# Summing the second layer's modulation with GpSimd beside a dense feed-forward

## The reference, cut to what matters

```python
c_act = jax.nn.silu(c)
for layer in range(DEPTH):                                   # DEPTH = 2
    mod = c_act @ mod_w[layer] + mod_b[layer]                # 1024 x 6144
    sh_m, sc_m, gt_m, sh_f, sc_f, gt_f = jnp.split(mod[:, None, :], N_MOD, axis=-1)
    h = x * (1 + sc_m) + sh_m
    ...                                                      # mixers (S5, GLA), w_out
    x = _layer_norm(DN_ALPHA * x + (1 + gt_m) * y, ln_mix_g[layer], ln_mix_b[layer])
    h = x * (1 + sc_f) + sh_f
    ...                                                      # layer 0: dense feed-forward; layer 1: 8 experts
    x = _layer_norm(DN_ALPHA * x + (1 + gt_f) * f, ln_ffn_g[layer], ln_ffn_b[layer])
```

## Time and profile before

| what | value |
|---|---|
| runs, not profiled | 2794.58 us median of 3 (2790.40 to 2800.55) |
| the profiled execution, first to last instruction | 2788.6 us |
| PE busy in it | 2530.0 us (91%) |
| DVE busy | 2080.7 us (75%) |
| ACT busy | 1461.2 us (52%) |
| POOL busy | 18.0 us (1%), 24 of its 29 instructions in the mixers |
| mean granted TensorE clock | 0.948 |

### The profile page before, as it was taken

How to read it: one execution, slowest core, us unless ns; L and a number is a source line. 1 busy time by engine, 2 the same in 40 slices (tenths; PEclk the granted TensorE clock), 3 DMA queues, 4 the chain that set the end, 5 groups by cost and what they waited for, 6 DMA issues and landing times.

```text
span 2788.6 us, 32539 instructions
## 1 busy us (share of the span) xinstructions
PE 2530.0 (91%) x12413; PEld 2026.9 (73%) x12413; DVE 2080.7 (75%) x2254; ACT 1461.2 (52%) x1535; POOL 18.0 (1%) x29
## 2 busy tenths in 40 slices
PE   5989689998686999999999999998888999988998
PEld 2736567777455788888888888876777887767787
DVE  5588787665766899989898988997865554776554
ACT  1221433442233777777777787775544544454543
POOL 0001000000000000000000000000000000000000
PEclk9997899998697999999999999999989999999999
DMA  7451246654132899999999999995403553503452
GB/s 239 154 184 66 91 171 250 243 211 127 46 121 76 307 356 360 347 361 356 345 361 372 371 358 355 359 348 191 139 31 106 166 187 110 196 1 106 136 183 89
DMA packets 274343, 598.12 MB, mean 214 GB/s; under 512 B 28722, under 2 KB 37248, under 8 KB 273026
## 3 DMA queue, kind: packets, MB, share of 16 engines
q1 hardware_dynamic: 252144, 580.30, 58.7%
q10 hardware_dynamic: 22034, 15.67, 2.0%
HBM read 594.87 MB, written 1.06 MB: 214 GB/s over the span
## 4 chain that ended last, share of the span: by engine, by line
PE 64%; DVE 26%; ACT 4%; issue 2%; ACTq 2%; DMA 2%; DVEq 0%; POOLq 0%
PE PS L215 62%; DVE WL L171 6%; PE PS L237 2%; DVE MW L171 2%; DVE WF L171 2%; DVE AR L171 2%; ACTq L150 2%; ACT WH L207 2%; DVE MOD L171 1%; DVE HF L171 1%; DVE H L171 1%; DVE SMALL L182 1%; DVE AR L179 1%; DVE HTR L171 1%; ACT AR L207 1%
## 5 line engine op out<-in xcount | busy, mean ns | idle before, releaser
L171 DVE TENSOR_TENSOR WL<-RG,WH 128x1024 fp32r<-128x1024 f32 (+1 forms) x558 | 919.2, 1647 | 371.2 <-ACT WH L207 339.0
L207 ACT ACTIVATE WH<-RG 128x1024 fp32r<-128x1024 f32 (+1 forms) x558 | 781.7, 1401 | 615.4 <-PE PS L215 552.7
L215 PE MATMUL PS<-WH,HTR 128*128 128x512 f32 (+2 forms) x2920 | 847.6, 388 | 40.9 <-DVE HTR L171 13.7
L215 PEld LDWEIGHTS PS<-WH,HTR 128*128 128x128 f32 x2920 | 551.3, 191 | 154.5 <-DVE HTR L171 15.3
L215 PE MATMUL PS<-WL,HTR 128*128 128x512 f32 (+2 forms) x1460 | 506.8, 385 | 1.4 <-DVE WL L171 1.4
L215 PE MATMUL PS<-WH,ATR 128*128 128x512 f32 x1624 | 457.9, 394 | 17.5 <-DVE WL L171 9.4
L215 PEld LDWEIGHTS PS<-WH,ATR 128*128 128x128 f32 x1624 | 305.9, 189 | 82.6 <-DVE WL L171 16.0
L215 PE MATMUL PS<-MW,HTR 128*128 128x512 f32 x1332 | 330.0, 395 | 1.0 <-DVE MW L171 0.5
L215 PEld LDWEIGHTS PS<-WL,HTR 128*128 128x128 f32 x1460 | 279.0, 191 | 55.5 <-DVE WL L171 2.7
L215 PEld LDWEIGHTS PS<-MW,HTR 128*128 128x128 f32 x1332 | 244.5, 188 | 55.3 <-DVE MW L171 6.5
L171 DVE TENSOR_TENSOR MW<-RG,MW 128x2048 fp32r<-128x2048 f32 x112 | 256.8, 2292 | 12.5 <-ACT MW L207 0.6
(11 more groups left out here) (230 smaller groups left out, 1993.9 us busy)
## 6 DMA issues: line engine op xcount, KB each, us to landing
RG<-in_moe_w_gate SPq DMA_DIRECT2D x112, 1024.0 KB, 6.9
RG<-in_moe_w_up SPq DMA_DIRECT2D x112, 1024.0 KB, 6.7
RG<-in_moe_w_down SPq DMA_DIRECT2D x112, 1024.0 KB, 6.8
RG<-in_w_ff SPq DMA_DIRECT2D x64, 1024.0 KB, 5.0
RG<-in_mod_w SPq DMA_DIRECT2D x48, 1024.0 KB, 5.2
RG<-in_w_in SPq DMA_DIRECT2D x34, 1024.0 KB, 6.1
RG<-in_w_out SPq DMA_DIRECT2D x16, 1024.0 KB, 5.1
RG<-in_ffn_w_gate SPq DMA_DIRECT2D x14, 1024.0 KB, 5.2
```

Of the source, the lines that this page charges most:

```text
L171: return self.did(lambda: self.e.tensor_tensor(o, a, b, op))
L207: return self.did(lambda: self.e.activation(o, a, f, bias=bias, scale=scale))
L215: return self.did(lambda: self.e.matmul(o, l, r, start=start, stop=stop))
```

## The change

- `plan_sums` now plans 24 raw loads, i = 0..11 with two k each: i 0 to 3 are columns 0:2048, i 4 to 7 columns 3072:5120, i 8 to 11 the two gate rows. `SUMS_BY` puts one pair behind gate n and one pair behind up n in each of the blocks 1 to 6.
- The eight loads (`plan_mod(1, 6, 10)`), the 64 matmuls, the ACT copy, the transposes and DVE's finish of them leave the second mixers.
- `g_sums` runs on POOL beside the feed-forward. For each load it multiplies the ring slot in place by c_act[k] (tensor_scalar) and adds the slot to the sum (tensor_tensor). In the first load of columns one multiplication writes the sum itself. For the gate rows both steps are done twice, on 1024 columns each.
- DVE does no sums any more. PE's 16 matmuls of one column come twice, in blocks 3 and 6 (`COLUMNS_BY`), and DVE adds the bias (`v_sums`) before the low parts of down n-1; ACT's part (`a_sums`) is gone. POOL waits for the first of these before it writes HROW again.

```diff
-        SUMS_BY = (), (0,), (1, 2), (3,), (4, 5), (6,), (7,)
+        SUMS_BY = (), (0, 1), (2, 3), (4, 5), (6, 7), (8, 9), (10, 11)
+        COLUMNS_BY = {3: 0, 6: 1}
...
-            else:
-                plan_mod(1, 6, 10)
...
                         W.plan(("gate", n), w["ffn_w_gate"][0][:, n * 512:(n + 1) * 512], 8, 512)
+                        for i in SUMS_BY[n][:1]:
+                            plan_sums(i)
                         W.plan(("up", n), w["ffn_w_up"][0][:, n * 512:(n + 1) * 512], 8, 512)
-                        for i in SUMS_BY[n]:
+                        for i in SUMS_BY[n][1:]:
                             plan_sums(i)
...
-        def v_sums(v, i):
-            g = i // 4
-            v.wait_ge(sums_in, 3)
-            for k in (i % 4 * 2, i % 4 * 2 + 1):
-                ld = W.of["sums", i, k][0]
-                v.wait_ge(W.landed[ld.slot], ld.use)
-                for m, at in enumerate(SUMS_AT[g]):
-                    x = v.stt(at, ld.dst[:, m, :], sm(24 + k, 1), at, MUL, ADD)
-                x.then_inc(W.raw_added)
+        def g_sums(g):
+            for at in SUMS_AT[2]:
+                x = g.ms(at, 0.0)
+            x.then_inc(sums_g, "clear")
+            for i in range(12):
+                if i == 4:
+                    g.wait_ge(sums_pe, 0, "cols0")
+                if i == 8:
+                    g.wait_ge(sums_in, 2)
+                for k in (i % 4 * 2, i % 4 * 2 + 1):
+                    ld = W.of["sums", i, k][0]
+                    g.wait_ge(W.landed[ld.slot], ld.use)
+                    for m, at in enumerate(SUMS_AT[i // 4]):
+                        if i < 8 and k == 0:
+                            x = g.ts(at, ld.dst[:, m, :], sm(24 + k, 1), None, MUL)
+                        else:
+                            g.ts(ld.dst[:, m, :], ld.dst[:, m, :], sm(24 + k, 1), None, MUL)
+                            x = g.tt(at, at, ld.dst[:, m, :], ADD)
+                    x.then_inc(W.raw_added)
...
+        def v_sums(v, i):
+            a_ = 48 + 24 * i
+            v.wait_ge(sums_pe, 0, f"cols{i}")
+            v.tt(MC[:, a_:a_ + 16], PS[:, 5, 0:16], MB[:, a_:a_ + 16], ADD).then_inc(sums_v, f"cols{i}")
+            v.ts(MC[:, a_ + 8:a_ + 16], MC[:, a_ + 8:a_ + 16], 1.0, None, ADD)
...
             if l:
                 yield from pe_row_sums(pe)
-                yield
-                pe.wait_ge(sums_v, 0, "row3")
-                yield from pe_mod(pe, 6)
```

More of the change, by code:

```diff
@@ L686, in pe_sums @@
-        def pe_sums(pe, ready):
-            pe.wait_ge(*W.of["sums", 3, 7][0].raw)
+        SUMS_AT = (HROW,), (HROW,), (GTM, ROWT)
+        def a_sums_in(a):
+            a.wait_ge(sums_g, 0, "clear")
+            for (c, n), at in zip(ROWS_AT, SUMS_AT[2]):
+                a.dma(at[0:1, :], w["mod_b"][1:2, c:c + n]).then_inc(sums_in)
+        def g_sums(g):
[17 more added lines that the diff above has]
+                    x.then_inc(W.raw_added)
@@ L689, in pe_sums @@
+        def pe_sums(pe, i, ready):
+            pe.wait_ge(*W.of["sums", 4 * i + 3, 7][0].raw)
             ready()
@@ L691, in pe_sums @@
                 x = pe.mm(PS[:, 5, j:j + 1], HROW[:, j * 128:(j + 1) * 128], COL[:, 1:2], True, True)
-            x.then_inc(sums_pe)
-        def a_sums(a):
-            a.wait_ge(sums_pe, 1)
-            a.act(MC[:, 48:56], PS[:, 5, 0:8], ACT.Copy)
-            a.act(MC[:, 56:64], PS[:, 5, 8:16], ACT.Identity, bias=1.0).then_inc(sums_a)
+            x.then_inc(sums_pe, f"cols{i}")
+        def v_sums(v, i):
[3 more added lines that the diff above has]
+            v.ts(MC[:, a_ + 8:a_ + 16], MC[:, a_ + 8:a_ + 16], 1.0, None, ADD)
         ROW_SUMS = [(GTM, GTM, h) for h in range(2)] + [(ROWT, GTF, h) for h in range(2)]
@@ L1501, in v_mods @@
                 yield from v_row_sums(v)
-            for i in ((6,) if l else range(1, 6)):
+            for i in (() if l else range(1, 6)):
                 yield
                 v_mod(v, i)
-                if i in (3, 6):
-                    v_ln_cols(v, l, 8 * l, 16 + 8 * l, 4)
+                if i == 3:
+                    v_ln_cols(v, 0, 0, 16, 4)
         def nothing(*_):
@@ L1526, in a_mixers @@
         def a_mixers(a, l):
-            weave(a, f"mixers{l}", s=a_s5(a, l), g=a_gla(a, l), m=once(lambda: a_mod(a, 6 if l else 3)),
+            weave(a, f"mixers{l}", s=a_s5(a, l), g=a_gla(a, l), m=iter(()) if l else once(lambda: a_mod(a, 3)),
                   b=once(lambda: (a_second_in(a), a_ln_rows(a, 1, "mix", 1))) if l else once(lambda: a_s5_in(a, 1)))
@@ L1817, in a_ffn_ln, with pe_ffn @@
             run(roots)
-        def pe_ffn(pe, gate, up, down, nblk, r0, ready, sums=None):
+        def pe_ffn(pe, gate, up, down, nblk, r0, ready, sums=()):
             for n in range(nblk):
@@ L1825, in pe_ffn @@
                         pe.wait_ge(ffn_a, r - 1, f"sg{t}")
-                beside = n == sums
                 pe_up(pe, W.of[gate(n)], 4, ready,
-                      (lambda: pe_sums(pe, lambda: pe.wait_ge(ffn_v, r - 1, "lo0"))) if beside else None)
-                if beside:
-                    pe.wait_ge(sums_a, 1)
+                      (lambda: pe_sums(pe, sums[n], lambda: pe.wait_ge(ffn_v, r - 1, "lo0"))) if n in sums else None)
+                if n in sums:
+                    pe.wait_ge(sums_v, 0, f"cols{sums[n]}")
                 if n:
@@ L3337, in v_beside @@
                 run(rest, 2)
+            if n in COLUMNS_BY:
+                v_sums(v, COLUMNS_BY[n])
             if n == 5:
-                v.wait_ge(sums_a, 1)
                 v_ln_cols(v, 1, 32, 48, 1)
-            for i in SUMS_BY[n]:
-                v_sums(v, i)
+            if n == 6:
+                v_ln_cols(v, 1, 8, 24, 4)
         def a_beside(a, n):
```

26 lines of the change are left out of this document (8 added, 18 removed).

## The result

| | before | after |
|---|---|---|
| runs, median of 4 each | 2797.57 us (2790.40 to 2802.09) | 2892.93 us (2891.24 to 2900.84) |
| profiled span | 2788.6 us | 2899.0 us |
| mean granted TensorE clock | 0.948 | 0.921 |
| feed-forward, from its first matmul to the first GTF product of the layer norm | 264.9 us | 362.6 us |
| from there to the first matmul of the experts' weights (the second mixers and what lies around them) | 208.4 us | 212.1 us |

The kernel is slower, by a ratio of 1.035 [1.0327, 1.0373]. The direction is the forecast one, the size is not: 2893 against 2815, and outside the range, which ended at 2856. The first stage has +97.7 us where +27 stood in the prediction, the second +3.7 where -6 stood. The medians differ by 95.4; the profiled execution of after was the slowest of its four.

The account below looks back on a forecast made before the run. PE, 91% busy, bounded the kernel; POOL was to bound blocks 3 to 6. Span 2788.6 + 27 (feed-forward, removal included) - 6 (second mixers) = 2809.6 us, median 6.0 above: 2815 us, range 2774 to 2856.

Parts of the forecast that it names:

- multiplications near 2.4: Sign in the feed-forward: POOL's in-place multiplication of 2048 columns takes 2.4 us, half of the addition.
- the layer norm near 644: Sign: the first GTF product of the layer norm comes near 644 us on the trace, against 617.2 before.
- the mixers shorter: Sign in the second mixers: the chain's second stretch of PE is shorter by 8 us.
- the third rival: Feed-forward: low parts wait on POOL and PE stalls within every matrix, or multiplication as dear as addition: 2855 us; chance 0.20.
- T: POOL's time per raw load, multiplication and addition over 2048 columns: 7.0 us, between 3.6 and 11.8.
- The addition: POOL's tensor_tensor addition of 2048 columns in the feed-forward: 4.6 us, between 2.35 and 5.9.
- The exclusion: A DVE instruction with two SBUF inputs and a POOL instruction block each other for their whole length.
- The steady block: Blocks 3 to 6: POOL's four loads 28 us, collisions 10.4, landing 5.2; taken as 42.5 us against PE's 34.
- Blocks 1 and 2: S5 pieces on DVE wait for POOL: PE 14 us late in block 1, up 2 another 17, the old stall gone.
- Removal (a): Feed-forward: taking all sums off DVE saves PE's stall, its cold clock and other waits, -12 us.
- The mixers: Second mixers: removing 64 matmuls gives -6 us, between -2 and -10, with 8 for the score steps and 1 to 2 us lost per cold gap.
- The first: Rival: POOL's work in the feed-forward is hidden, T up to 4.6 us, only the removals show: about 2775 us; chance 0.22.

Follow-up runs that it names:

- e3: The kernel after with POOL's multiplications and additions replaced by memsets that read no SBUF, raw loads and waits kept: 2821.49 us, ratio 1.0118.
- e4: The kernel after without the raw loads and without the sums on any engine: 2796.13 us, ratio 0.9998.
- its three likes: e4 with 128, 64 or 32 matmuls of unused result added in the second mixers: 2809.84, 2792.87 and 2792.93 us.
- e12: e4 with DVE's bias of the column sums moved between the second and third low part of up n: 2786.44 us, ratio 0.997.
- e15: e4 with 64 matmuls of unused result where the removed ones stood in the second mixers: 2792.87 us, ratio 0.9984.
- e1: The kernel after with POOL's 22 multiplications left out, additions kept: 2830.85 us, ratio 1.0151.
- e10: The kernel after with POOL's multiplication as a tensor_tensor with c_act[k] broadcast: 2884.19 us, ratio 1.0342.
- e2: The kernel after without the 24 raw loads, POOL's multiplications and additions run on its own sum tiles: 2847.66 us, ratio 1.0211.
- e17: The kernel after with POOL multiplying only the first half of the columns, by a broadcast tensor_tensor: 2844.23 us, ratio 1.0155.
- e11: The kernel after with POOL multiplying only the first half of the columns, by tensor_scalar: 2835.23 us, ratio 1.0132.

## Why the prediction was right or wrong

**The direction** was right, and by the mechanism named: POOL becomes the bound of blocks 3 to 6, with raw loads waiting in SP's queue and PE short of low parts. The signs that the prediction asked for are there: POOL busy 252 us in the feed-forward, additions of 4.54 us and more, low parts of 2.13 us, a clock under 0.94 from 352 on. The signs that failed are "multiplications near 2.4", the layer norm near 644 (715.5), and the mixers shorter.

**The step that failed** is the size of the multiplication: "it reads one input and not two, so I take half of the addition, 2.4". It is 5.44 us, dearer than the addition. The bounds (1.2 to 5.9) held it, and the third rival named just this ("the multiplication is as dear as the addition") at 0.20; it asked for 2855. With T = 10.0 the prediction's own sum gives 22 x 3.0 = 66 more, +93 for the feed-forward against the measured +97.7; how much luck is in that is said below. The halving had no row behind it. The only row of both kinds was DVE's (0.694 for the tensor_scalar, 1.225 for the tensor_tensor); that ratio of 0.57 belongs to DVE and doesn't carry over.

**The addition**, 4.6 us worked out from DVE's fixed part and POOL's 0.72 for 256 columns, came out at 4.54. The Trainium skill (GPSIMD Engine Reference, 3.1 Elementwise) has 4.497 us for it, and the trace agrees; for the multiplication by a scalar of the partition the run measures 5.44 us, above the 1.8 to 3.1 that the prediction estimated from that section's 1.03 to 1.8 cycles per element for simple loops, and the measurement decides.

**The exclusion** was right for tensor_tensor and too strong for POOL's tensor_scalar (inside one, DVE ended a low part 0.66 us before it). The Trainium skill (SBUF — State Buffer, Who interferes with whom) has the second comer blocked for the full instruction; with POOL's additions the trace agrees (1.1 us behind their end), for its tensor_scalar it does not. That section also has a DVE tensor_scalar in a two-port mode contend; the trace shows one of 0.69 us taking 5.82 beside POOL, though not its mode. A POOL instruction without a read, e3's memset, holds no low part (1226 ns in the mean).

**The steady block** was put at 42.5 us and took 49.9; with T = 10.0 the same formula gives 40 + 10.4 + 5.2 = 55.6. The landing was right: POOL stood for 5.0, 5.7 and 5.4 us at the head of blocks 4, 5 and 6. The term that was too dear is the collisions. In these blocks POOL's instructions are stretched by 4.9, 4.1 and 4.5 us in all, and with 0.9 to 1.6 of pauses between them that is some 6 in place of 10.4: an instruction stretched by low parts costs POOL 0.5 to 0.8 us more and not 1.3 (4.54 became 5.07, 5.44 became 6.23). Blocks 4 and 5 take 51.4 and 52.6 us on POOL; block 3 takes 43.5, as one of its loads has no addition and some of its instructions met no low part.

**Blocks 1 and 2** were put at +22 (14 + 17, less the 9 of the old stall) and gave +40: 19 in block 1 for 14, and 21 in block 2 for 8. Seven pieces of S5 in block 2 took 27 us (447.5 to 474.6), about one per POOL instruction as the step said, but at 10.0 us a load; PE's wait there was 26.3 us, where up 2 was to be 17 late.

**A wait that was put at nothing** is POOL's for the first column matmuls. The prediction has POOL start block 3 at 479, when the ninth load lands. It landed at 490.9, and POOL started at 509.9, behind PE. Followed along POOL, the layer norm's 71 us of delay against 644.5 are 12 for that landing, 19 for this wait, 30 from there to the last raw load (195 us in place of 165) and 10 behind it. So the +93 is near +97.7 in part by luck: steady blocks too dear, the start of block 3 too early. No run takes the wait away, so what it is worth alone is open.

**Removal (a)** was put at -12 and is -4.1 in e4, -1.6 to -2.3 in its three likes. 4.8 us of the missing 8 are the bias of the two column rounds, which was costed at nothing because PE's other waits would hide it; e12 gets them back. The rest was not traced.

**The mixers** were put at -6, and the removal gave nothing: -8 for the steps was -3.1, since behind the second gap the clock stayed at its lower level through all four steps and not for 1 to 2 us, and the stretch behind them took 3.9 more. e15 shows it from the other side: its steps take 19.0 us, and its stage ends as e4's.

**The rivals.** The first set its point at T up to 4.6: e1, with T at 4.5, is 31.5 us slower in the stage, so a POOL that just fits into the block still costs, since its reads hold DVE (1816 ns a low part). (Its 2775 also takes 8 us for the mixers where the forecast takes 6.) The third was nearest, by its second condition. Its first condition, PE stalled by low parts within every matrix, didn't come: PE waited 14 times for a low part in 21 matrices of four parts each, once for 26 us.

## What to carry to other kernels

An idle GpSimd beside a DVE that is bound is not free room: price its instructions by a row of the same operation at the same size, and where there is none keep the dearest bound, for a multiplication by a scalar is no half of an addition. Then count twice, once for the ring slots it holds and once for the DVE instructions it holds; here the engine that looked full did the same sums for a third of the loss. Ask as well what the added engine itself must wait for: here it was PE, which that engine had made late. And a stretch of matmuls beside other engines' work may be worth nothing when it is removed, since the gap that it leaves cools PE for the work behind.

## What was not expected of the hardware

- POOL, 128 partitions of float32: tensor_tensor 4.54 us for 2048 columns and 2.34 for 1024; with one operand a broadcast scalar 3.60 and 1.89 (e10), and the same two numbers where both inputs are one tile (e2); tensor_scalar 5.44 and 2.85; memset 1.81 and 0.95. The two-input addition is cheaper than the one-input product by a scalar of the partition, and the same product is cheaper as a tensor_tensor.
- A tensor_scalar of POOL lets a waiting DVE instruction through before it ends and is itself stretched (5.44 to 6.23 us); a tensor_tensor does not. The kind counts beside T: e17 (6.4) loses 4.9 us more in the feed-forward than e11 (7.4), in one trace each.
- POOL's memsets hold no low part of DVE: the 61 that begin inside one take 1226 ns in the mean and 1228 at most (e3).
